# Expert stage of a two-block model: where TensorE turns the rows of a chunk

## The reference, cut to what matters

```python
for e in range(N_EXPERTS):                    # 8 experts, D_FF_EXPERT = 3584
    y = y + gate[:, e:e + 1] * swiglu(xt, wg[e], wu[e], wd[e])
def swiglu(h, wg, wu, wd):
    return (jax.nn.silu(h @ wg) * (h @ wu)) @ wd
```

## Time and profile before

| what | value |
| --- | --- |
| median of 3 timed runs | 2464.31 us (2462.68 to 2464.95) |
| the profiled execution: its span, first to last instruction | 2461.3 us |
| the median less that span | 3.0 us |
| TensorE matmul busy | 2426.1 us, 99% of the span |
| VectorE busy | 2038.9 us, 83% |
| ScalarE busy | 1535.8 us, 62% |
| expert stage, first to last of its transpositions | 406.7 to 1356.6 us |

### The profile page before, as it was taken

How to read it: one execution, slowest core, us unless ns; L and a number is a source line. 1 busy time by engine, 2 the same in 40 slices (tenths; PEclk the granted TensorE clock), 3 DMA queues, 4 the chain that set the end, 5 groups by cost and what they waited for, 6 DMA issues and landing times.

```text
span 2461.3 us, 44012 instructions
## 1 busy us (share of the span) xinstructions
PE 2426.1 (99%) x17074; PEld 2210.0 (90%) x17074; DVE 2038.9 (83%) x2626; ACT 1535.8 (62%) x2090; POOL 174.7 (7%) x244
## 2 busy tenths in 40 slices
PE   9999999999999999999999999999999999999999
PEld 9999998899999998888898899988899899988998
DVE  5688866888988899999998799786898898787665
ACT  5644565777777777878776644557544544567543
POOL 2111021000000000000010111011011011010000
PEclk9999999999999999999999999999999999999999
DMA  7698554999999999999999688443687587432541
GB/s 295 229 366 309 201 185 157 398 365 384 370 382 369 383 378 394 394 390 392 385 391 372 239 319 308 158 148 127 245 319 295 220 316 293 152 129 82 218 181 76
DMA packets 136637, 696.20 MB, mean 283 GB/s; under 512 B 16528, under 2 KB 16656, under 8 KB 87728
## 3 DMA queue, kind: packets, MB, share of 16 engines
q1 hardware_dynamic: 109872, 598.79, 64.5%
q0 software_dynamic: 23424, 88.16, 9.3%
q10 hardware_dynamic: 3136, 6.43, 0.7%
HBM read 683.29 MB, written 13.24 MB: 283 GB/s over the span
## 4 chain that ended last, share of the span: by engine, by line
PE 83%; DVE 7%; ACT 4%; DMA 4%; issue 2%; POOL 0%; SPq 0%; ACTq 0%; DVEq 0%; POOLq 0%
PE ps L2460 16%; PE ps L2056 15%; PE ps L2057 14%; PE ps L2058 14%; PE ps L2627 9%; PE ps L2462 8%; DMA ring<-wstream 4%; DVE w_parts L1745 2%; DVE w_parts L1358 1%; PE ps L2592 1%; PE ps L2085 1%; PE ps L2081 1%; ACT w_parts L1147 1%; DVE a_parts L1752 1%; ACT w_parts L824 1%
## 5 line engine op out<-in xcount | busy, mean ns | idle before, releaser
L2460 PE MATMUL ps<-a_parts,w_parts 128*128 128x512 f32 x1760 | 618.9, 393 | 1.5 <-DVE a_parts L1323 1.3
L2056 PE MATMUL ps<-w_parts 128*112 128x256 f32 x1792 | 520.9, 291 | 8.9 <-DVE w_parts L1745 7.8
L1745 DVE TENSOR_TENSOR w_parts<-ring,w_parts 128x2048 fp32r<-128x2048 f32 x222 | 506.4, 2281 | 0.0
L2058 PE MATMUL ps<-w_parts 128*112 128x256 f32 x1792 | 499.0, 278 | 0.0
L2057 PE MATMUL ps<-w_parts 128*112 128x256 f32 x1792 | 499.0, 278 | 0.0
L2462 PE MATMUL ps<-a_parts,w_parts 128*128 128x256 f32 x1760 | 492.7, 280 | 0.0
L1147 ACT ACTIVATE w_parts<-ring 128x2048 fp32r<-128x2048 f32 x222 | 424.3, 1911 | 18.5 <-DMA ring<-wstream 18.3
L2460 PEld LDWEIGHTS ps<-a_parts,w_parts 128*128 128x128 f32 x1760 | 329.8, 187 | 75.5 <-issue 3.7
L2056 PEld LDWEIGHTS ps<-w_parts 128*112 128x112 f32 x1792 | 313.4, 175 | 45.3 <-issue 38.8
L2462 PEld LDWEIGHTS ps<-a_parts,w_parts 128*128 128x128 f32 x1760 | 332.3, 189 | 0.0
L2057 PEld LDWEIGHTS ps<-w_parts 128*112 128x112 f32 x1792 | 312.9, 175 | 6.5
(11 more groups left out here) (288 smaller groups left out, 4390.1 us busy)
## 6 DMA issues: line engine op xcount, KB each, us to landing
ring<-wstream SPq DMA_DIRECT2D x378, 1024.0 KB, 7.8
ring<-wstream SPq DMA_DIRECT2D x378, 512.0 KB, 5.9
proj<-astream POOLq DMA_DIRECT2D x144, 512.0 KB, 5.6
slot_rows<-branch POOLq DMA_DIRECT2D x7, 448.0 KB, 7.2
slot_out<-slot_rows POOLq DMA_DIRECT2D x1, 3136.0 KB, 14.8
sq<-slot_rows ACTq DMA_DIRECT2D x49, 64.0 KB, 5.2
slot_out<-pT ACTq DMA_DIRECT2D x49, 64.0 KB, 4.8
vtok<-crow POOLq DMA_DIRECT2D x3, 512.0 KB, 3.8
```

The source lines that it names most:

```text
L1745: nc.vector.tensor_tensor(up_lo[:, n % 2, :], ring[:, s, 0:UP], up_hi[:, n % 2, :], ALU.subtract).then_inc(up_used, 1)
L2056: mm(o, stationary[0], moving[0], start=start, stop=False, skip_group_check=True)
L2058: return mm(o, stationary[1], moving[0], start=False, stop=stop, skip_group_check=True)
L2460: mm(ps[:, bank, :], hi, a_parts[:, :, k, :], start=k == 0, stop=k == KB - 1, skip_group_check=True)
```

## The change

The transposition of chunk n - 1 is issued ahead of all 24 products of `up(n)`, in place of behind its first two blocks of three. Nothing else changes: the same instructions run, on the same data, and the last transposition of all stands alone as before.

```diff
                 def up(n, r, first=False):
 
                     b, n_e = n % 2, n // FX
+                    if not first:
+                        turn(n - 1, r)
                     pe.wait_ge(xmul_ready, r * FX + (n + 1))
                     for k in range(KB):
                         if k % 4 == 0:
...
-                        if k == 2 and not first:
-                            turn(n - 1, r)
                         at = slice(k * T, (k + 1) * T)
```

## The result

| | median of 6 runs | lowest to highest | span of the profiled run |
| --- | --- | --- | --- |
| before | 2463.09 us | 2461.49 to 2464.95 | 2461.3 us |
| after | 2470.19 us | 2468.9 to 2471.1 | 2467.4 us |

The ratio is 1.0032, 95% interval 1.0022 to 1.0042: the change makes the kernel 7.1 us slower by the medians, 6.1 us by the profiled spans. That is inside my range and 1.7 us above my number of 2468.5; its sign at the 0.2% bound is "slower", to which I had given 0.38.

The account below looks back on a forecast made before the run. TensorE bounds full experts; a three-engine loop, or transfers at c = 14 to 19, bounds few-row ones. Terms 0.2 + 0 + 2.95 + 0.3 + 0.7 = 4.15, say +4.2, on 2464.3 gave 2468.5 us, range 2463.0 to 2473.8.

Parts of the forecast that it names:

- slower: Whole kernel: slower by more than the 0.2% bound, 4.9 us; chance 0.38.
- Few-row experts, place and mechanism: Experts 4 to 6, steady chunks: transposition waits for L1834, nothing passes it; loop 0.08 us longer, 0.04 per chunk.
- Few-row borders: c = 19 to c = 3 of the next expert: no transfer waited for, delays stay; three borders, sum 2.95 us.
- What the transfers take up: Few-row experts, c = 4 to 18: 1.8 us on the loop hidden by 10.3 us of transfer waits; counted 0.
- nothing takes the delays up: Rival for experts 4 to 6 and expert 0: each delay is passed on, together 7.2 us; chance 0.28.
- Full experts, steady: TensorE reaches the transposition after L1834 ended, so no wait; cost 0, with 0.2 us for single late chunks in experts 1 to 3.
- Expert 0: Two waiting transpositions cost 0.70 us more each, later transfer waits take up 1.4; 0.3 us left, upper bound 1.5.
- no term: TensorE's granted clock: 1.00 (the 2.4 GHz level) in all windows by expert, so counted as nothing.
- Expert 7: From c = 19 VectorE sets the pace; six products lost as cover put TensorE back once, 0.7 us.
- The sum: All terms together: 4.15 us, say +4.2 us, a small loss below the 4.9 us bound.
- the forecast's own range: Whole kernel: 2466.8 to 2470.3 us, for the forecast case of +2.5 to +6 us; chance 0.48.

Follow-up runs that it names:

- e6: Kernel before, with half of each up tile's transfer left out in experts 4 to 6 (does not compute the layer): median 6.1 us below before.
- e7: Changed kernel (transposition first), with half of each up tile's transfer left out in experts 4 to 6 (does not compute the layer): 4.6 us above before.
- e3: Changed kernel, but expert 0 keeps the transposition behind the sixth up product: median 8.1 us above before.
- e5: Changed kernel plus five extra matmuls ahead of the transpositions of expert 0's chunks 2 and 5: median 7.6 us above before.
- e9: Changed kernel plus five extra matmuls ahead of expert 0's chunk 2 transposition alone: median 7.1 us above before.
- e2: Kernel before, with the transposition first in few-row experts 4 to 6 only: median 2.9 us above before.
- the light pair: e6 and e7, both with smaller up transfers in experts 4 to 6, differing only in the transposition's place: medians 6.1 us below and 4.6 us above before.
- e11: Kernel before, with VectorE's up subtraction in two halves; transposition behind the sixth product in experts 1 to 3, the twelfth elsewhere: 2.7 us below before, ratio 0.9988.
- e12: Changed kernel (transposition first), with VectorE's up subtraction in two halves: median 11.6 us above before.
- e8: Kernel before, with VectorE's up subtraction in two halves and the transposition behind the twelfth product in every chunk: 3.5 us below before, ratio 0.9986.
- e10: Kernel before, with the transposition behind the twelfth product in every chunk and the up subtraction in one piece: median 90.1 us above before.
- e1: Kernel before, with the transposition first in the five full experts only: median 5.0 us above before.

## Why the prediction was right, and where it was not

- **Few-row experts, place and mechanism: right.** The transposition waits in 77 chunks and follows L1834 by 0.06 us, nothing passes it, 2.88 us follow to the down products. The loop grew by 0.11 us where I had 0.08, and c = 4 to 13 by 0.66 an expert (0.066 a chunk, not 0.04, so the cost of a steady chunk was too low). e6 and e7 give the same at these chunks without waits for transfers, 0.51 to 0.66.
- **Few-row borders: right in kind, near in size.** c = 20 to 27 plus c = 0 to 3 of the next are 0.57 + 0.25, 0.58 + 0.14 and 0.67 + 0.57, in all 2.8 us against 2.95. The same sum is 3.4 to 3.6 in e3, e5 and e9, and 3.8 from e6 to e7.
- **What the transfers take up: right in kind, under-sized.** I had 1.8 us going into waits of 10.3. The waits fell by 5.3 us, not by the 1.8 I wrote, and by 2.4 to 6.0 in e2, e3, e5 and e9; the light pair puts the cost without them at 6.2 us and what is taken up at 1.8 to 3.8. Under the rival "nothing takes the delays up" experts 4 to 6 should have lost 4.75 us; in three runs they lost 2.4 to 2.6, in two others (e2, e3) 3.75 and 4.48, which comes near it. So the amount is not the same in every run, and that much stays open.
- **Full experts, steady: wrong.** "Cost 0" is the step that failed. I named it as what would refute me, and 28 chunks took 120.8 us where I had 120.0. Not by a wait, and not by a transposition that costs more behind 512-column products, which I had named as the possible reason: a short chunk takes 4.21 to 4.22 us as before. TensorE's products step by 113.5 or 118 ns, in many chunks the longer step begins at the transposition, and six more products now stand behind it. I had worked with one step of 0.116 for all and did not look at the alternation of 4.29 and 4.21 us, which stood in the trace of before. 1.75 against 0.2 us. The order of before alone spreads from -0.57 to +0.46 in these experts (e2, e11, e6), and no run with the transposition first is below +1.35.
- **Expert 0: wrong by a term I had ruled out.** I read a clock of 1.00 in all windows and wrote that it is no term. It held for before. The change lengthens one idle stretch from 1.83 to 2.51 us, and the clock fell behind it; 1.2 of expert 0's 1.66 us is that (e7 and e9, where it did not fall). The rest, 0.46, is near my 0.3. The Trainium skill (TensorE: Matmul & The Clock Gate, "HAM oscillation — how this bites in real kernels") describes kernels whose waits let the clock drop, so that the work behind each wait starts slow. This trace agrees, with one such wait: 15 or so products at 0.21 us. In e7 and e12 the same wait was not followed by a fall.
- **Expert 7: not decided.** 0.30 in place of 0.7, but 0.83, 0.75 and 0.94 in e3, e5 and e9, which have the same code there.
- **The sum:** 4.15 against 6.34 us. Experts 0 to 3 missed by 2.9 us, few-row experts and expert 7 were 0.7 too high. The median, 2470.19 us, lies just inside the forecast's own range (up to 2470.3 us). That is luck in part: the errors have both signs, and the range did not know of the clock and of the product's step.

## What to carry to other kernels

A step that waits for another engine belongs behind as much independent work as its consumers leave room for. Here the room has two edges: with no work ahead of it TensorE waits in full view (part of the +7 us), six products later than before its consumers starve (+90 us); an order that looks free in steady chunks must be read at both. Before a "no wait here, so no cost" is written, look for a pattern in the lengths of chunks that nothing waits in. And a clock that reads 1.00 in one kernel says nothing of a changed one with a longer idle stretch: there the clock can be a term again.

The gain lay in what TensorE waited for: splitting VectorE's subtraction, so that the first half of the products can start early, with the transposition behind the twelfth product, was worth 3 us (e8, e11). Neither part does it alone: the place without the halves costs 90 us (e10), the halves with the transposition first 11.6 (e12); the halves with the order of before in experts 4 to 6 were not run.

## What the runs showed of the hardware that was not expected

- A gap of 2.51 us in TensorE's work was followed by 3 us at a granted clock of 0.50 in two kernels (the change, e1). Gaps of 2.49 (e7) and 2.44 us (e12) at the same place were not, nor was one of 1.83, nor one of 0.32 us with extra matmuls ahead of it (e9). Such a fall is a chance, not a certainty, and cost expert 0 1.2 us.
- Products of 256 columns step by about 113.5 or by 118 ns at a granted clock of 1.00, and the longer step can begin at a transposition among them and last to the end of the chunk (38 of 84 chunks before, 49 in e8). The Trainium skill (TensorE: Matmul & The Clock Gate, "Wait — 56ns, not 53.3ns?") gives N / 2.4 GHz and about 2.5 ns; by it 256 columns would be an estimated 109 ns. No run here shows 109, and the page names no second step.
- The core loaded weights at 396 to 398 GB/s in the windows 892 to 1006 and 1006 to 1121 us of e8, where ScalarE waited for them; the changed kernel's 387 to 390 are therefore not what the transfers can do at most. Nor are 398: at 428 to 436 us the kernel before moved 427.
